# Scan core of a Mamba-2 layer: exponents four heads ahead, token tiles turned among the states

## The chip, the cores and the metric

The kernel runs on one core of one Trainium2 chip. The metric is the device time of one execution in microseconds (us), median of three runs; less is better. Engines are called PE (TensorE, matmuls and transposes), DVE (VectorE), ACT (ScalarE), POOL (GpSimd) and SP (SyncE, which here only issues DMAs). Each engine works through its own instructions in the order in which they are written; engines wait for one another by semaphores.

## What is computed

The program is a two-layer backbone over 256 latent tokens and 256 context tokens of width 1024 with SwiGLU feed-forward blocks around a mixer. The change lies in the mixer of the second layer alone, a bidirectional Mamba-2 scan:

```
x, B, C, dt = project(a)                 # 2048, 8*128, 8*128, 64 columns
a_cs        = cumsum(dt * A)             # per head and direction, 32 heads
cb          = C @ B^T                    # per group (8 groups of 4 heads), token x token
y_diag      = (cb * exp(segsum(a))) @ x  # inside the latent tokens
states      = B^T @ (x * decay_to_end)   # of the context tokens, carried over
y_off       = C @ states * exp(a_cs)
y           = y_diag + y_off + D * x     # then gated, normed, projected
```

## The kernel before

All arithmetic is fp32; large projections are split into a high and a low part. The program is written out engine by engine, and each engine's order is fixed by hand. The part around the change is called the core here, and has two parts.

**Ahead of the heads (L2157 to L2197 on PE).** `turn_x(x)` turns one tile of x (four 128x128 transposes) into a bank; tiles 0 to 7 are context, 8 to 15 latent tokens. `turn_b` does the same for B. DVE's `token_major(x)` (L1553) scales a turned tile twice, once for each direction, into `xtok`. `states(c4)` (L2152) makes the context states of two of the eight groups, and ACT copies them out to `ssb` (L978). Tiles 8 to 15 overwrite the place of tiles 0 to 7, so `token_major(8 + i)` waits for the states that read tile i. `b_dot_c(g)` (L2180, L2181) is B times C of a group; DVE masks two quarters of it (L1566, L1567). In the order before, all eight groups of states come first, then tiles 8 and 9 and B times C of group 0; tiles 10 to 15 are turned in the first three groups of heads, one for each pair.

**The heads (L2198 to L2226 on PE).** 32 heads in 8 groups of 4, two heads (a pair) at a time, 16 pairs. For a head h

- SP loads two rows of decays, each broadcast to 128 partitions (256 KB): `afb` (L591), from which the exponents are made, and `csx` (L582; by the buffer's name also `tt` or `pp`), which carries the states.
- DVE's `exponents(h)` makes two quarters `dm` from `afb` (L1577, L1578). It runs two heads ahead: `exponents(h + 2)` follows `products(h)`.
- ACT takes four exponentials into `ee` (L1006 to L1012).
- DVE's `products(h)` multiplies them with B times C (L1588, L1589) into `mm`, and then, once in a group, multiplies y of the group before with its gate (`gate_y`, L1600).
- POOL multiplies `csx` with C (L1741).
- PE adds for each pair D times x (L2206), the states (L2211) and the products (L2217 to L2223) in one bank; after the first pair of a group it makes B times C of the next group and sums squares of an earlier one (L2189).

Buffers: four `afb`, two `dm`, four `ee`, four `mm`, eight `csx`. SP's queue holds the two kinds of rows in turns: after `afb` of head h comes `csx` of head h + 3 (`CS_AHEAD = 3`). A `csx` row from head 8 on takes the buffer of head h - 8, and so waits until PE has done L2211 of that head's pair (`cs_used`, counted in pairs):

```
def decay_rows(h):
    if h >= 2 * HPG:
        sp.wait_ge(cs_used, h // 2 - HPG + 1)
    sp.dma_start(csx[cs_slot(h)]...)
```

An `afb` row from head 4 on waits for exponents and exponentials of head h - 4 (`d_done`, `e_done`).

Of the kernel before, what the change touches and what calls it, by code (L numbers as in the profile page):

```python
# [5 lines left out]
F32 = mybir.dt.float32  # L6
# [123 lines left out]
def build(nc, t, out, kscr, afscr, cscr):  # L130
# [39 lines left out]
    with ExitStack() as ctx:  # L170
# [17 lines left out]
        def sem(name):  # L188
            return ctx.enter_context(nc.semaphore(name))
# [63 lines left out]
        mm_ = [core(f"mm{i}", [3 * L]) for i in range(HPG)]  # L253
        afb = [core(f"afb{i}", [2, L]) for i in range(HPG)]
        dm = [core(f"dm{i}", [2 * P]) for i in range(2)]
        mask = core("mask", [3, P])
        btok = at("btok", [P, 2, D], F32, o_w)
        tt = [sb(f"tt{i}", [NT]) for i in range(4)]
# [134 lines left out]
        s_mask = sem("s_mask")  # L393
        afb_in = [sem(f"afb_in{i}") for i in range(HPG)]
        cb_mm = sem("cb_mm")
# [41 lines left out]
        def turned_x(x):  # L437
            return x % 4 if x < 8 else 0 if x == 8 else 7

# [11 lines left out]
        def _(sp):  # L451
# [135 lines left out]
            for h in range(HEADS):  # L587
                if h >= HPG:
                    sp.wait_ge(d_done, h - 3)
                    sp.wait_ge(e_done, h - 3)  # L590
                sp.dma_start(afb[h % HPG][:], afscr[0, h].partition_broadcast(P)).then_inc(afb_in[h % HPG], 16)  # L591
                if h + CS_AHEAD < HEADS:
                    decay_rows(h + CS_AHEAD)

            begin(MBOUT)
            for j in range(DT):
                sp.wait_ge(w_lo, MBOUT.w - 1 + j)
                if j == 1:
                    sp.wait_ge(cs_used, HEADS // 2 - 2)
                load(MBOUT.raw + j, mbo_v[:, :, j * P:j * P + P], 16, P)  # L600
# [15 lines left out]
        def _(act):  # L616
# [353 lines left out]
            for b in range(4):  # L970
                act.wait_ge(tb_mm, b + 1)
                if b == 0:
                    act.dma_start(mask[:].rearrange("p a n -> p (a n)"), t["c_mask"]).then_inc(s_mask, 16)
                act.activation(btok[:, b // 2, (b % 2) * 512:(b % 2) * 512 + 512], bank[6 + b % 2][:],
                               ACT.Copy).then_inc(tb_out, 1)
            for g in range(GROUPS):
                act.wait_ge(st_mm, g + 1)
                act.activation(ssb[:, :, g * 256:g * 256 + 256], bank[4 + g % 2][:].rearrange("p (a n) -> p a n", a=2),  # L978
                               ACT.Copy).then_inc(st_out, 1)
            act.wait_ge(af_st, 64)  # L980

# [13 lines left out]

            d_x(0)
            for h in range(HEADS):
                g, r = h // HPG, h % HPG
                d_ = dm[h % 2]
                if r == 1 and g + 1 < GROUPS:  # L1000
                    d_x(g + 1)
                act.wait_ge(afb_in[r], 16 * g + 16)
                if g:
                    act.wait_ge(m_done, h - 3)

                act.activation(ee[r][:, P:2 * P], afb[r][:, 0, P:L], ACT.Exp, bias=tk[:, 0, h:h + 1])  # L1006
                act.activation(ee[r][:, 2 * P:3 * P], afb[r][:, 1, 0:P], ACT.Exp, bias=tk[:, 1, HEADS + h:HEADS + h + 1])
                if g and r == 3:
                    square_y(g)
                act.wait_ge(d_done, h + 1)  # L1010
                act.activation(ee[r][:, 0:P], d_[:, 0:P], ACT.Exp, bias=tk[:, 0, HEADS + h:HEADS + h + 1])
                act.activation(ee[r][:, 3 * P:4 * P], d_[:, P:2 * P], ACT.Exp,  # L1012
                               bias=tk[:, 1, HEADS + h:HEADS + h + 1]).then_inc(e_done, 1)
            act.activation(rs[:, 24:25], eps[:], ACT.Sqrt)
            act.wait_ge(raw_in[MBOUT.raw % 2], 16 * (MBOUT.raw // 2 + 1))
# [27 lines left out]
        def _(dve):  # L1043
# [526 lines left out]
            def exponents(h):  # L1570

                g, r = h // HPG, h % HPG
                af, d_ = afb[r], dm[h % 2]
                dve.wait_ge(afb_in[r], 16 * g + 16)
                if h >= 2:
                    dve.wait_ge(e_done, h - 1)
                dve.scalar_tensor_tensor(d_[:, 0:P], af[:, 0, 0:P], tkd[:, 0, h:h + 1], af[:, 1, 0:P], ALU.add, ALU.min)  # L1577
                dve.scalar_tensor_tensor(d_[:, P:2 * P], af[:, 0, P:L], tkd[:, 1, h:h + 1], af[:, 1, P:L],  # L1578
                                         ALU.add, ALU.min).then_inc(d_done, 1)
# [26 lines left out]
            own.sync()  # L1606
            exponents(0)
            exponents(1)
            token_major(8)
            token_major(9)  # L1610
            b_dot_c(0)
            for h in range(HEADS):
                products(h)
                g, r = h // HPG, h % HPG
                if r % 2 and g < 3:
                    token_major(10 + 2 * g + r // 2)
                if r == 1 and g:
                    gate_y(g)
                if h + 2 < HEADS:
                    exponents(h + 2)  # L1620
                if r == 2 and g + 1 < GROUPS:
                    b_dot_c(g + 1)
# [40 lines left out]
        def _(pool):  # L1663
# [88 lines left out]
        def _(pe):  # L1752
# [377 lines left out]
            def turn_x(x):  # L2130

                seg, c4, T = 1 - x // 8, x % 8 // 2, x % 2
                if x >= 10:
                    pe.wait_ge(tr_out, x)
                elif x >= 4:
                    pe.wait_ge(tr_out, x - 3)
                elif T == 0:
                    pe.wait_ge(z_free, ZP.zf + 14 + x)
# [22 lines left out]
            pe.wait_ge(tb_out, 4)  # L2161
            for c4 in range(4):
                if 1 <= c4 < 3:
                    turn_x(2 * c4 + 2)
                    turn_x(2 * c4 + 3)
                states(c4)
            turn_x(8)
            turn_x(9)
            pe.wait_ge(st_out, GROUPS)
            pe.wait_ge(tk_out, 1)  # L2170

            def b_dot_c(g):

                if g:
                    pe.wait_ge(cb_out, g)
                whole = bank[1 + g % 2]
                for T in range(2):
# [182 lines left out]
```

## Time and profile before

| | us |
|---|---|
| median of 3 runs (lowest, highest) | 2005.96 (2005.37, 2007.53) |
| span of the profiled execution | 2002.1 |
| core ahead of the heads, in that span | 1644 to 1671.7 |
| the heads, in that span | 1671.7 to 1741 |

The profiled execution is told by its span, first instruction to last; the median of the runs is 3.9 us above it, which is what lies around the span and what runs differ by. Times of single instructions below are starts in us from the span's start. A matmul's duration is partly modelled and overlaps the next one's, so work on PE is measured from start to start. In an instruction row, xN is the count that was merged, and the bracket tells idle time of the engine ahead of it and what ended it.

### The profile page before, as it was taken

To read this page: it belongs to the slowest core of one execution; us is meant where nothing else is said; L and a number is where in the kernel's file an instruction comes from. 1 tells how busy PE (TensorE), PEld (TensorE's weight loads), DVE (VectorE), ACT (ScalarE), POOL (GpSimd) and SP (SyncE) were. 2 spreads that over 40 slices of the span, in tenths; PEclk is the share of its full clock that TensorE was granted. 3 is DMA by queue.
4 is the path that set the end of the run, shared out by engine and by line. 5 is a ranking of instruction groups with operands and counts; after the bars stand their busy time and mean duration, and the time that the engine had idled before them with its cause. 6 is when DMAs were issued, how large, how long until landed. Compare 5 with 4: busy or idle time off the path is not lost. (4 is left out here: it accounts for less than half of the span.)

```text
span 2002.1 us, 24595 instructions
## 1 busy us (share of the span) xinstructions
PE 1956.0 (98%) x9953; PEld 1631.5 (81%) x9953; DVE 1288.1 (64%) x1797; ACT 715.2 (36%) x1007; POOL 212.0 (11%) x151
## 2 busy tenths in 40 slices
PE   7999999999999999999999999999999998999998
PEld 4788888878888878888888888888888996688897
DVE  5755546678788576554767555466776578947654
ACT  4522222242311332223224222222434545735542
POOL 1000000100065200000110000001000003530001
PEclk9999999999999999999999999999999999999999
DMA  9544435543440254442655443355443445655554
GB/s 365 203 150 147 132 107 179 166 151 106 169 163 1 84 189 145 150 147 80 197 154 174 152 147 128 111 174 171 141 139 114 147 143 163 207 169 169 189 161 135
DMA packets 279302, 306.46 MB, mean 153 GB/s; under 512 B 9459, under 2 KB 249748, under 8 KB 277398
## 3 DMA queue, kind: packets, MB, share of 16 engines
q1 hardware_dynamic: 275398, 293.57, 46.0%
q10 hardware_dynamic: 3792, 11.33, 1.5%
q8 instruction: 78, 1.28, 0.3%
q14 instruction: 34, 0.28, 0.0%
HBM read 298.44 MB, written 6.43 MB: 152 GB/s over the span
## 5 line engine op out<-in xcount | busy, mean ns | idle before, releaser
L1756 PE MATMUL banks<-xhl,wh 128*128 128x512 f32 (+1 forms) x1756 | 664.9, 379 | 6.8 <-DVE xhl L1129 2.4
L1758 PE MATMUL banks<-xhl,wl 128*128 128x512 f32 (+1 forms) x1756 | 662.2, 377 | 0.0
L1757 PE MATMUL banks<-xhl,wh 128*128 128x512 f32 (+1 forms) x1756 | 662.1, 377 | 0.0
L1049 DVE TENSOR_TENSOR wl<-raw,wh 128x2048 fp32r<-128x2048 f32 (+2 forms) x193 | 398.7, 2066 | 236.8 <-ACT wh L622 231.5
L622 ACT ACTIVATE wh<-raw 128x2048 fp32r<-128x2048 f32 (+1 forms) x200 | 347.1, 1735 | 538.6 <-PE banks L1758 477.8
L1756 PEld LDWEIGHTS banks<-xhl,wh 128*128 128x128 f32 x1756 | 331.1, 189 | 75.7 <-DVE xhl L1129 5.7
L1758 PEld LDWEIGHTS banks<-xhl,wl 128*128 128x128 f32 x1756 | 331.0, 188 | 60.7
L1757 PEld LDWEIGHTS banks<-xhl,wh 128*128 128x128 f32 x1756 | 331.0, 189 | 59.2
L1756 PE MATMUL banks<-gh,wh 128*128 128x512 f32 (+1 forms) x704 | 255.4, 363 | 3.8 <-DVE wl L1049 3.8
L1757 PE MATMUL banks<-gl,wh 128*128 128x512 f32 (+1 forms) x704 | 255.2, 362 | 0.0
L1758 PE MATMUL banks<-gh,wl 128*128 128x512 f32 (+1 forms) x704 | 255.2, 362 | 0.0
L1194 DVE TENSOR_TENSOR pp<-tt,banks 128x512 f32<-128x512 f32 x66 | 42.4, 684 | 173.0 <-PE banks L1758 173.0
L1756 PEld LDWEIGHTS banks<-gh,wh 128*128 128x128 f32 x704 | 132.9, 189 | 24.9 <-issue 2.5
L1758 PEld LDWEIGHTS banks<-gh,wl 128*128 128x128 f32 x704 | 132.9, 189 | 20.7
L1757 PEld LDWEIGHTS banks<-gl,wh 128*128 128x128 f32 x704 | 132.9, 189 | 20.4
L1674 POOL MEMSET acc<- 128x512 f32 x6 | 3.2, 529 | 1150.7 <-DVE gl L1163 905.7
L1762 PE MATMUL banks<-xhl,wh 128*128 128x512 f32 x348 | 121.5, 396 | 0.8 <-DVE xhl L1129 0.8
L1680 POOL TENSOR_TENSOR acc<-acc,tt 128x512 f32<-128x512 f32 (+1 forms) x41 | 83.4, 2034 | 365.4 <-ACT tt L745 303.2
L695 ACT ACTIVATE tt<-banks 128x512 f32<-128x512 f32 x66 | 35.9, 596 | 239.3 <-PE banks L1758 239.2
L1763 PE MATMUL banks<-xhl,wl 128*128 128x256 f32 x348 | 96.5, 277 | 0.0
L1148 DVE SCALAR_TENSOR_TENSOR hT<-banks,mods,hT 128x256 f32<-128x256 f32 x64 | 28.7, 480 | 101.6 <-PE banks L1758 101.6
L1063 DVE SCALAR_TENSOR_TENSOR banks<-ada_rawo,cb 128x1024 f32<-128x1024 f32 x48 | 81.8, 1705 | 3.4 <-DMA ada_rawo<-in_ada_rest 3.4
(281 smaller groups left out, 2069.9 us busy)
## 6 DMA issues: line engine op xcount, KB each, us to landing
raw<-in_ffn_in SPq DMA_DIRECT2D x88, 1024.0 KB, 5.1
raw<-in_ffn_out SPq DMA_DIRECT2D x64, 704.0 KB, 4.6
ada_rawf<-in_ada_rest SPq DMA_DIRECT2D x60, 512.0 KB, 3.4
ada_rawo<-in_ada_rest SPq DMA_DIRECT2D x48, 512.0 KB, 3.3
raw<-in_mb_in_w SPq DMA_DIRECT2D x24, 1024.0 KB, 5.4
raw<-in_hy_in_w SPq DMA_DIRECT2D x12, 1024.0 KB, 5.2
afb<-decays SPq DMA_DIRECT2D x32, 256.0 KB, 3.8
raw<-in_mb_out_w SPq DMA_DIRECT2D x8, 1024.0 KB, 6.1
```

What stands on the lines that cost most here:

```text
L622: return act.activation(wh[n % 2][:, 0:cols], raw[r_slot][:, 0:cols], ACT.Copy).then_inc(w_hi, 1)
L695: act.activation(tt[u][:, 0:n], bank[u][:, 0:n], ACT.Silu).then_inc(gate_ready, 1)
L1049: dve.tensor_tensor(wl[n_slot][:, 0:cols], raw[r_slot][:, 0:cols], wh[n_slot][:, 0:cols].bitcast(F32), ALU.subtract).then_inc(w_lo, 1)
L1063: own(dve.scalar_tensor_tensor(banks[free][:].rearrange("p a n -> p (a n)"), pieces[i][:], half, cb0[:], ALU.mult, ALU.mult, accum_out=mod ...
L1148: ins = dve.scalar_tensor_tensor(x, bank[4 + um][:, w * L:w * L + L], mods[layer][:, i * 2 + (DT * k5 + um), w:w + 1], x, ALU.mult, ALU.add)
L1194: dve.tensor_tensor(pp[(pi.q + u) % 2][:, 0:n], tt[u][:, 0:n], acc[:, u * n:u * n + n] if n == L else bank[2 + u][:, 0:n], ALU.mult).then_ ...
L1680: pool.tensor_tensor(acc[:, 0:n], acc[:, 0:n], tt[um][:, 0:n], ALU.add).then_inc(acc_done, 1)
L1756: pe.matmul(dst, h, x_hi, start=start, stop=False)
L1757: pe.matmul(dst, h, x_lo, start=False, stop=False)
L1758: return pe.matmul(dst, l_, x_hi, start=False, stop=stop)
L1762: pe.matmul(b[:, 0:2 * L], wh[wslot][:, lo:lo + P], xhl[:, :, k, 0:L], start=k == 0, stop=False)
L1763: return pe.matmul(b[:, 0:L], wl[wslot][:, lo:lo + P], xh[:, k, 0:L], start=False, stop=k == DT - 1)
```

## The change

- `afb` gets eight buffers and `dm` four. `exponents(0)` to `exponents(3)` come ahead of the heads, and `exponents(h + 4)` follows `products(h)`. An `afb` row waits for head h - 8 instead of h - 4; the row of head 4 waits until tile 7 of x is turned, since its buffer lies where context x stood. `CS_AHEAD` and SP's order of rows stay.
- PE turns tiles 8 to 13 and makes B times C of group 0 among the states; only tiles 14 and 15 are left in group 0 of the heads. DVE scales them in the same order. Banks of the turned tiles and the waits for them change with it (`BANK_READ`).
- ACT takes the exponentials of head 0 and `d_x(0)` before the last two copies of states. POOL's `csx` product waits for the exponents of head h instead of h - 2, which is the same place in DVE's order.
- `btok` stands in a `raw` buffer, so the first load of the output projection waits for the last states.

```diff
         afb = [core(f"afb{i}", [2, L]) for i in range(HPG)]
+        afb += [at(f"afb{HPG + i}", [P, 2, L], F32, big + (24 + 2 * i) * KB) for i in range(HPG)]
         dm = [core(f"dm{i}", [2 * P]) for i in range(2)]
+        dm += [at(f"dm{2 + i}", [P, 2 * P], F32, big + (32 + i) * KB) for i in range(2)]
...
-        btok = at("btok", [P, 2, D], F32, o_w)
+        btok = at("btok", [P, 2, D], F32, o_raw + MBOUT.raw % 2 * 8 * KB)
...
         def turned_x(x):
-            return x % 4 if x < 8 else 0 if x == 8 else 7
+            return x % 4 if x < 8 else (0, 7, 2, 7, 0, 2, 7, 7)[x - 8]
+
+        BANK_READ = {8: 5, 10: 7, 11: 10, 12: 9, 13: 11, 14: 12, 15: 15}
...
             for h in range(HEADS):
-                if h >= HPG:
-                    sp.wait_ge(d_done, h - 3)
-                    sp.wait_ge(e_done, h - 3)
-                sp.dma_start(afb[h % HPG][:], afscr[0, h].partition_broadcast(P)).then_inc(afb_in[h % HPG], 16)
+                if h == HPG:
+                    sp.wait_ge(tr_mm, 8)
+                if h >= 2 * HPG:
+                    sp.wait_ge(d_done, h - 7)
+                    sp.wait_ge(e_done, h - 7)
+                sp.dma_start(afb[h % (2 * HPG)][:], afscr[0, h].partition_broadcast(P)).then_inc(afb_in[h % (2 * HPG)], 16)
                 if h + CS_AHEAD < HEADS:
                     decay_rows(h + CS_AHEAD)
...
+                if j == 0:
+                    sp.wait_ge(st_mm, GROUPS)
...
+            exponentials(0)
+            state_out(GROUPS - 2)
+            d_x(0)
+            state_out(GROUPS - 1)
+            for h in range(1, HEADS):
+                exponentials(h)
...
             def exponents(h):
-                dve.wait_ge(afb_in[r], 16 * g + 16)
-                if h >= 2:
-                    dve.wait_ge(e_done, h - 1)
+                dve.wait_ge(afb_in[h % (2 * HPG)], 16 * (h // (2 * HPG)) + 16)
+                if h >= HPG:
+                    dve.wait_ge(e_done, h - 3)
...
-            exponents(0)
-            exponents(1)
+            for h in range(HPG):
+                exponents(h)
             token_major(8)
             token_major(9)
+            token_major(10)
+            token_major(11)
             b_dot_c(0)
+            token_major(12)
+            token_major(13)
             for h in range(HEADS):
                 products(h)
                 g, r = h // HPG, h % HPG
-                if r % 2 and g < 3:
-                    token_major(10 + 2 * g + r // 2)
+                if r % 2 and g == 0:
+                    token_major(14 + r // 2)
                 if r == 1 and g:
                     gate_y(g)
-                if h + 2 < HEADS:
-                    exponents(h + 2)
+                if h + HPG < HEADS:
+                    exponents(h + HPG)
...
-                    pool.wait_ge(d_done, h - 1)
+                    pool.wait_ge(d_done, h + 1)
...
-            for c4 in range(4):
-                if 1 <= c4 < 3:
-                    turn_x(2 * c4 + 2)
-                    turn_x(2 * c4 + 3)
-                states(c4)
-            turn_x(8)
-            turn_x(9)
-            pe.wait_ge(st_out, GROUPS)
-            pe.wait_ge(tk_out, 1)
+            states(0)
+            turn_x(4)
+            turn_x(5)
+            states(1)
+            for x in range(6, 10):
+                turn_x(x)
+            states(2)
+            turn_x(10)
+            turn_x(11)
...
             b_dot_c(0)
+            states(3)
+            turn_x(12)
+            turn_x(13)
+            pe.wait_ge(st_out, GROUPS)
+            pe.wait_ge(tk_out, 1)
...
-                    if g < 3:
-                        turn_x(10 + 2 * g + p)
+                    if g == 0:
+                        turn_x(14 + p)
```

What the change makes of the order on two engines follows. First SP's queue from the row of head 3 on, before (L591 is `afb`, L582 the other kind; the names number the buffers):

```order
L591 DMA afb3_108<-decays 128x512
L582 DMA pp0_119<-decays 128x512
L591 DMA afb0_105<-decays 128x512 [waits e_done,d_done]
L582 DMA pp1_120<-decays 128x512
L591 DMA afb1_106<-decays 128x512 [waits e_done,d_done]
L582 DMA csx0_121<-decays 128x512 [waits cs_used]
L591 DMA afb2_107<-decays 128x512 [waits e_done,d_done]
L582 DMA csx1_122<-decays 128x512 [waits cs_used]
L591 DMA afb3_108<-decays 128x512 [waits e_done,d_done]
```

and the same stretch after (L597 is `afb`, L586 the other kind):

```order
L597 DMA afb3_108<-decays 128x512
L586 DMA pp0_125<-decays 128x512
L597 DMA afb4_109<-decays 128x512 [waits tr_mm]
L586 DMA pp1_126<-decays 128x512
L597 DMA afb5_110<-decays 128x512
L586 DMA csx0_127<-decays 128x512 [waits cs_used]
L597 DMA afb6_111<-decays 128x512
L586 DMA csx1_128<-decays 128x512 [waits cs_used]
L597 DMA afb7_112<-decays 128x512
```

The rows of heads 4 to 7 lose their waits for earlier heads; the place of every row, and the wait for `cs_used` ahead of head 6, stay.

DVE at heads 3 to 5, before (L1588 and L1589 are the products, L1577 and L1578 the exponents, L1553 a tile of x):

```order
L1588 TENSOR_TENSOR mm3_104<-ee3_100,banks0 128x512 [waits e_done,cb_out]
L1589 TENSOR_TENSOR mm3_104<-ee3_100,banks1 128x256
L1553 TENSOR_TENSOR xtok_53<-banks3,tk_155 128x512 [waits tr_mm,st_mm]
L1553 TENSOR_TENSOR xtok_53<-banks3,tk_155 128x512
L1577 SCALAR_TENSOR_TENSOR dm1_110<-afb1_106,tkd_156 128x128 [waits e_done,afb_in1]
L1578 SCALAR_TENSOR_TENSOR dm1_110<-afb1_106,tkd_156 128x128
L1588 TENSOR_TENSOR mm0_101<-ee0_97,banks1 128x512 [waits head_mm,e_done,cb_out]
L1589 TENSOR_TENSOR mm0_101<-ee0_97,banks1 128x256
L1577 SCALAR_TENSOR_TENSOR dm0_109<-afb2_107,tkd_156 128x128 [waits e_done,afb_in2]
L1578 SCALAR_TENSOR_TENSOR dm0_109<-afb2_107,tkd_156 128x128
L1588 TENSOR_TENSOR mm1_102<-ee1_98,banks1 128x512 [waits head_mm,e_done,cb_out]
```

and after (L1606 and L1607, L1595 and L1596, L1572):

```order
L1606 TENSOR_TENSOR mm3_104<-ee3_100,banks0 128x512 [waits e_done,cb_out]
L1607 TENSOR_TENSOR mm3_104<-ee3_100,banks1 128x256
L1572 TENSOR_TENSOR xtok_53<-banks3,tk_161 128x512 [waits tr_mm,st_mm]
L1572 TENSOR_TENSOR xtok_53<-banks3,tk_161 128x512
L1595 SCALAR_TENSOR_TENSOR dm3_116<-afb7_112,tkd_162 128x128 [waits e_done,afb_in7]
L1596 SCALAR_TENSOR_TENSOR dm3_116<-afb7_112,tkd_162 128x128
L1606 TENSOR_TENSOR mm0_101<-ee0_97,banks1 128x512 [waits head_mm,e_done,cb_out]
L1607 TENSOR_TENSOR mm0_101<-ee0_97,banks1 128x256
L1595 SCALAR_TENSOR_TENSOR dm0_113<-afb0_105,tkd_162 128x128 [waits e_done,afb_in0]
L1596 SCALAR_TENSOR_TENSOR dm0_113<-afb0_105,tkd_162 128x128
L1606 TENSOR_TENSOR mm1_102<-ee1_98,banks1 128x512 [waits head_mm,e_done,cb_out]
```

Between the products of heads 4 and 5 now stand the exponents of head 8, which read the row in `afb0`; before it was those of head 6.

## Rows read from the trace of the kernel before

**Rows 1.** The page's section 1, busy time of each engine
```profile
PE 1956.0 (98%) x9953; PEld 1631.5 (81%) x9953; DVE 1288.1 (64%) x1797; ACT 715.2 (36%) x1007; POOL 212.0 (11%) x151
```

**Rows 2.** Busy time by stage, over the heads; columns in the first line
```profile
core 0: us, PE busy (x) PEld busy (x) DVE busy (x) ACT busy (x) POOL busy (x), PEclk, DMA share, GB/s
...
1667.00:1740.00 73.00, 65.53 (x544) 42.87 (x544) 68.01 (x161) 53.73 (x153) 35.76 (x28) 0.98 0.70 220
```

**Rows 3.** Timeline of PE, heads: start, us, engine, line, op
```profile
1682.68 0.65 PE L2217 MATMUL banks<-mm,xtok 128*64 128x256 f32 x4 [1.06 <-DVE mm L1589]
...
1703.18 0.65 PE L2217 MATMUL banks<-mm,xtok 128*64 128x256 f32 x4 [1.37 <-DVE mm L1589]
...
1718.85 0.65 PE L2217 MATMUL banks<-mm,xtok 128*64 128x256 f32 x4
...
1723.63 0.60 PE L2217 MATMUL banks<-mm,xtok 128*64 128x256 f32 x4
...
1725.03 0.70 PE L2206 MATMUL banks<-xb,small 128*128 128x256 f32 x2
1725.66 1.08 PE L2211 MATMUL banks<-csx,ssb 128*64 128x256 f32 x8
1726.67 0.65 PE L2217 MATMUL banks<-mm,xtok 128*64 128x256 f32 x4
...
1728.12 0.49 PE L2180 MATMUL banks<-csb,xb 128*128 128x128 f32 x2
...
1729.93 0.68 PE L2206 MATMUL banks<-xb,small 128*128 128x256 f32 x2
```

**Rows 4.** Timeline of DVE: exponents 25, products 24, exponents 26, exponents 28
```profile
1723.26 0.34 DVE L1577 SCALAR_TENSOR_TENSOR dm<-afb,tkd 128x128 f32<-128x128 f32 x1
...
1723.78 0.68 DVE L1588 TENSOR_TENSOR mm<-ee,banks 128x512 f32<-128x512 f32 x1
...
1724.71 0.72 DVE L1577 SCALAR_TENSOR_TENSOR dm<-afb,tkd 128x128 f32<-128x128 f32 x1
...
1728.59 0.72 DVE L1577 SCALAR_TENSOR_TENSOR dm<-afb,tkd 128x128 f32<-128x128 f32 x1
```

**Rows 5.** Timeline of SP: the decays of head 30, then afb of head 28
```profile
1723.84 0.32 SPq L582 DMA_DIRECT2D pp<-decays  x1
1724.26 0.42 SPq L591 DMA_DIRECT2D afb<-decays  x1
```

**Rows 6.** Waits of SP's queue, 1640 to 1742: total, times, longest
```profile
SPq L582 <- PE banks L2211: 16.5, 10, 2.9
```

**Rows 7.** Transfers into afb, from issue to landing
```profile
DMA to landing us min/median/max: 3.1/3.8/7.1
```

**Rows 8.** Timeline of PE, ahead of the heads and at the first pair
```profile
1656.99 7.07 PE L2152 MATMUL banks<-xtok,btok 128*128 128x256 f32 x32
1663.90 1.04 PE L2140 MATMUL banks<-small,xb 128*128 128x128 f32 x8
1664.77 0.47 PE L2180 MATMUL banks<-csb,xb 128*128 128x128 f32 x2
...
1665.74 0.60 PE L2206 MATMUL banks<-xb,small 128*128 128x256 f32 x2
...
1671.67 1.12 PE L2217 MATMUL banks<-mm,xtok 128*64 128x256 f32 x4 [2.77 <-DVE mm L1589]
...
1674.43 0.80 PE L2180 MATMUL banks<-csb,xb 128*128 128x128 f32 x2
```

**Rows 9.** Timeline of DVE, ahead of the heads
```profile
1659.15 0.34 DVE L1577 SCALAR_TENSOR_TENSOR dm<-afb,tkd 128x128 f32<-128x128 f32 x1
...
1664.61 2.48 DVE L1553 TENSOR_TENSOR xtok<-banks,tk 128x512 f32<-128x512 f32 x4 [4.32 <-PE banks L2140]
1667.01 0.43 DVE L1566 TENSOR_TENSOR banks<-banks,mask 128x256 f32<-128x256 f32 x1
```

**Rows 10.** Busy time by stage, columns as in rows 2
```profile
1672.00:1673.00 1.00, 1.00 (x8) 0.65 (x6) 1.00 (x4) 0.25 (x1) 0.00 (x0) 0.50 0.76 203
```

More of the change, by code:

```diff
@@ L393, in build @@
         s_mask = sem("s_mask")
-        afb_in = [sem(f"afb_in{i}") for i in range(HPG)]
+        afb_in = [sem(f"afb_in{i}") for i in range(2 * HPG)]
         cb_mm = sem("cb_mm")
@@ L972, in _ @@
                 if b == 0:
+                    act.wait_ge(w_lo, ZP.w + 7)
                     act.dma_start(mask[:].rearrange("p a n -> p (a n)"), t["c_mask"]).then_inc(s_mask, 16)
@@ L975, in _, with state_out @@
                                ACT.Copy).then_inc(tb_out, 1)
-            for g in range(GROUPS):
+            def state_out(g):
                 act.wait_ge(st_mm, g + 1)
@@ L979, in _ @@
                                ACT.Copy).then_inc(st_out, 1)
+            for g in range(GROUPS - 2):
+                state_out(g)
             act.wait_ge(af_st, 64)
@@ L994, in d_x, with exponentials @@
                     act.activation(xb[:, 0, m, :], xb[:, 0, m, :], ACT.Copy, scale=dcol[:, m:m + 1]).then_inc(dx_done, 1)
-            d_x(0)
-            for h in range(HEADS):
+            def exponentials(h):
                 g, r = h // HPG, h % HPG
-                d_ = dm[h % 2]
+                d_, af = dm[h % HPG], afb[h % (2 * HPG)]
                 if r == 1 and g + 1 < GROUPS:
                     d_x(g + 1)
-                act.wait_ge(afb_in[r], 16 * g + 16)
+                act.wait_ge(afb_in[h % (2 * HPG)], 16 * (h // (2 * HPG)) + 16)
                 if g:
                     act.wait_ge(m_done, h - 3)
-                act.activation(ee[r][:, P:2 * P], afb[r][:, 0, P:L], ACT.Exp, bias=tk[:, 0, h:h + 1])
-                act.activation(ee[r][:, 2 * P:3 * P], afb[r][:, 1, 0:P], ACT.Exp, bias=tk[:, 1, HEADS + h:HEADS + h + 1])
+                act.activation(ee[r][:, P:2 * P], af[:, 0, P:L], ACT.Exp, bias=tk[:, 0, h:h + 1])
+                act.activation(ee[r][:, 2 * P:3 * P], af[:, 1, 0:P], ACT.Exp, bias=tk[:, 1, HEADS + h:HEADS + h + 1])
                 if g and r == 3:
@@ L1570, in exponents @@
             def exponents(h):
-                g, r = h // HPG, h % HPG
-                af, d_ = afb[r], dm[h % 2]
-                dve.wait_ge(afb_in[r], 16 * g + 16)
-                if h >= 2:
-                    dve.wait_ge(e_done, h - 1)
+                af, d_ = afb[h % (2 * HPG)], dm[h % HPG]
+                dve.wait_ge(afb_in[h % (2 * HPG)], 16 * (h // (2 * HPG)) + 16)
+                if h >= HPG:
+                    dve.wait_ge(e_done, h - 3)
                 dve.scalar_tensor_tensor(d_[:, 0:P], af[:, 0, 0:P], tkd[:, 0, h:h + 1], af[:, 1, 0:P], ALU.add, ALU.min)
@@ L2132, in turn_x @@
                 seg, c4, T = 1 - x // 8, x % 8 // 2, x % 2
-                if x >= 10:
-                    pe.wait_ge(tr_out, x)
-                elif x >= 4:
+                if x in BANK_READ:
+                    pe.wait_ge(tr_out, BANK_READ[x])
+                elif 4 <= x < 8:
                     pe.wait_ge(tr_out, x - 3)
-                elif T == 0:
+                elif x < 4 and T == 0:
                     pe.wait_ge(z_free, ZP.zf + 14 + x)
@@ L2175, in b_dot_c @@
                     pe.wait_ge(cb_out, g)
+                if g == 1:
+                    pe.wait_ge(tr_out, 14)
                 whole = bank[1 + g % 2]
```

## The prediction

> **What bounds the kernel now.** I read the page from its first section down. PE is busy 98% of the span [rows 1], so the program as a whole is bound by its matmuls, and almost no saving on another engine can show outside the few stretches in which PE waits. The core is one. Over the heads the stage table has PE at 65.5 and DVE at 68.0 of 73.0 us, ACT at 53.7, POOL at 35.8 [rows 2]: two engines nearly full, so neither the mean nor the busiest engine says what bounds it. The timelines do. From pair 10 to pair 12, one group of heads, PE takes 1726.67 - 1718.85 = 7.82 us with no idle bracket in its rows [rows 3]. In the early groups it takes longer: pair 2 to pair 6 are (1703.18 - 1682.68) / 2 = 10.25 us a group, and there PE waits for DVE's products, as the brackets of 1.06 and 1.37 us tell [rows 3]. What DVE has more in the first three groups is two tiles of x a group. One pair of tiles costs DVE 1667.01 - 1664.61 = 2.40 us, 1.20 each [rows 9]. So the early groups are bound by DVE, the late ones by DVE and PE alike, and 2.40 of the 10.25 us is what the change takes aim at.
>
> Behind both stands a third party, SP's queue. It spent 16.5 us, in 10 waits, on PE's state matmuls L2211 [rows 6], since the `csx` rows wait for them, and every `afb` row waits its turn behind a `csx` row. Today that costs nothing, and how narrowly is seen at head 28: the state matmuls of pair 11 end when its products start, at 1723.63 [rows 3]; SP issues the decays of head 30 at 1723.84 and `afb` of head 28 at 1724.26 [rows 5]; a median landing of 3.8 us later [rows 7] is 1728.06; DVE reads it at 1728.59 [rows 4]. 0.5 us is to spare.
>
> **The change part by part.** I write T(k) for the start of pair k's products on PE.
>
> *Ahead of the heads.* DVE makes four heads' exponents in place of two before tile 8: it starts them at 1659.15 [rows 9], one head is 1723.78 - 1723.26 = 0.52 us [rows 4], so it is free at 1661.2 in place of 1660.2, and tile 9 is scaled at 1663.6. PE needs that for tile 11 (its bank), then makes B times C of group 0 (1665.74 - 1664.77 = 0.97), two groups of states (a quarter of 1663.90 - 1656.99 each, 1.73, so 3.46) and turns tile 12 (an eighth matmul row of 0.87 for two, 0.44) [rows 8]: 1663.6 + 0.44 + 0.97 + 3.46 + 0.44 = 1668.9. DVE then scales tiles 12 and 13 (2.40), and makes products 0, exponents 4, products 1. Products are 1724.71 - 1723.78 = 0.93 [rows 4], so T(0) = 1668.9 + 2.40 + 0.93 + 0.52 + 0.93 = 1673.7, against 1671.67 [rows 8]: **+2.0 us**. ACT's reordered work (head 0's exponentials before the last copies) lies under the states, and costs nothing unless the copies delay PE; a copy is short against the 1.73 us of a state group.
>
> *Group 0 of the heads.* Before, T(0) to T(2) is 1682.68 - 1671.67 = 11.0 us [rows 3, 8]. After, DVE has four heads of 0.93 + 0.52, two tiles of 1.20, two masks (an estimate of 0.66, from 0.43 for one [rows 9] less what overlaps), and about 0.38 twice, where L1577 takes 0.72 and not 0.34 [rows 4]: 5.8 + 2.4 + 0.66 + 0.76 = 9.6 us, and behind it a first wait for `afb` of head 8 of up to 1 us, by the same sum as below. **-0.5 us**, between -1.4 and +2.
>
> *Groups 1 to 7, the term that decides.* Two tiles a group less in groups 1 and 2 would save 2.4 us each. But moving exponents two heads up in DVE's order, without moving the `afb` rows up in SP's, moves the reader before the transfer. Exponents 28 should now follow products 24, at 1724.71 [rows 4], while the row lands at 1728.1. Behind it in DVE's queue stand products 25, and PE's pair 12 waits for those. The loop that closes is: state matmuls of pair k end; +0.21 and +0.42 until SP has issued `csx` and started `afb` of head 2k + 6 [rows 3, 5]; +3.8 to landing [rows 7]; +0.52 exponents, +0.93 products of head 2k + 3 [rows 4]; so T(k + 1) comes 5.9 us after. Then PE's products of a pair, 1728.12 - 1726.67 = 1.45, B times C and sum of squares, 1729.93 - 1728.12 = 1.81, and D times x and states of pair k + 2, 1726.67 - 1725.03 = 1.64 [rows 3], and the next loop begins. Together **10.8 us a group**, against 7.82. (This holds for odd k, whose T(k + 1) opens a group; for even k PE has reached its states early enough, while it waited, that nothing is added.)
>
> In groups 1 and 2, before 10.25 each, the saved tiles and the new wait cancel: 10.8 each, less 0.8 of the 1.81 once, because only from group 2 on squares are summed: **+0.3 us** for both. From T(6) to T(12), three groups, it is 3 x (10.8 - 7.82) = **+8.9 us**. I temper it to +8, because a stretched loop has fewer transfers in flight and the landing then tends to its minimum, 3.1 us [rows 7]: the bounds are 10.1 us a group, +6.8, and 10.8, +8.9. After T(12) exponents are done but for heads 30 and 31, and nothing is added or saved.
>
> The Trainium skill, in "DMA: Bandwidth & Descriptors" (Anatomy of one DMA), has a fixed cost of about 2.0 us and then bytes by 436 GB/s, an estimate of 2.6 us for 256 KB; by that the loop were 9.6 us and this term +5.3. The landing that the profile has, 3.8 with a minimum of 3.1, decides.
>
> *TensorE's clock.* Ahead of T(0) PE is idle for 2.77 us [rows 8], and right after the granted clock is 0.50, the 1.2 GHz level [rows 10]: pair 0's products take 1674.43 - 1671.67 = 2.76 in place of 1.45. After, every group holds 10.8 - 7.8 = 3 us of idle in one piece, ahead of its first pair. One such fall costs 1.3 us in the products and some 0.4 in what follows; between none and one in each of six groups, 0 to +9; I take two: **+3 us**. The Trainium skill describes this in "TensorE: Matmul & The Clock Gate" (HAM oscillation): a loop whose matmuls are short beside the transfer wait finds the clock low in every round. By that it would be six falls, a rival below.
>
> *The rest.* The first load of the output projection, at 1729 before, can only come earlier; its reader comes after the heads. POOL's product stays at the same place of DVE's order. `btok` in another buffer and the banks cost nothing. All that follows the heads moves with them.
>
> **The sum**: 2.0 - 0.5 + 0.3 + 8 + 3 = +12.8 us on the span of 2002.1, so 2014.9, and with the 3.86 us by which the median of the runs lies above the span, 2018.8.
>
> **Rivals.**
> 1. *Faster: the tiles' time shows and the rows are in time.* The place is groups 1 and 2, 2 x 2.4 = 4.8 us less, group 0 -1.4, ahead of the heads +2.0: -4.2, 2001.8. For it: PE did wait there for DVE. It decides if the new wait costs less than 4.2 / 3 = 1.4 us in each of the last three groups, which needs landings within about 2.2 us of issue, or `afb` issued 1.6 us sooner. Against: the minimum of 32 is 3.1. Chance 0.06.
> 2. *No change.* The two cancel, with a gain of some 4 us given back: 2006. It needs the in-between of the above. 0.05.
> 3. *The clock falls in every group*: 2.0 - 0.5 + 0.3 + 8 + 9 = +18.8, 2024.8. For it: idle pieces of 3 us, where 2.77 sufficed once. Against: with 1.06 and 1.37 us nothing fell, and part of a fall hides in the wait that follows. 0.24.
> 4. *The clock never falls, and landings are short*: 2.0 - 1.0 - 0.5 + 6.8 = +7.3, 2013.3. 0.20.
> 5. *The change doesn't do what it says*: eight `afb` buffers don't bring rows earlier, because `cs_used` gates the queue. That is part of my forecast.
>
> **How the numbers follow.** Forecast 2018.8 with 0.45; rivals 3 and 4 with 0.24 and 0.20; 0.11 for the first two. The range goes from 2011, a little under rival 4, to 2026, a little over rival 3. About 4 us, 0.2%, is what a measurement of this kernel can tell from no change. Slower by more than that 0.89, same 0.05, faster 0.06.
>
> **What would show it.** Right: DVE idle ahead of L1595 until a DMA into `afb` lands, 2 to 4 us once a group from group 2 on; PE idle ahead of L2246 by some 3 us at the first pair of a group; T(6) to T(12) some 32 us in place of 23.5; T(0) near 1673.7; SP's waits for L2240 far over 16.5 us. Wrong: no DVE wait for a DMA, or a group of heads at 7.8 us. Were T(0) to T(6) shorter by 4 us and the rest unchanged, rival 1 holds.

## The result, and the profile after

| | before | changed |
|---|---|---|
| median on one chip, 6 runs each (lowest, highest), us | 2005.66 (2003.67, 2007.53) | 2019.48 (2014.87, 2026.96) |
| ratio, with its 95% interval | | 1.0075 (1.0058 to 1.0092) |
| span of the profiled execution (its run) | 2002.1 | 2015.6 (2017.41) |

The change makes the kernel slower, by 13.8 us (0.69%) between the medians and by 0.75% by the ratio. The forecast was 2018.8 in 2011 to 2026. All ratios are of fast runs alone: one slow execution of the kernel before, 3281.98 us at a granted clock of 0.56, taken beside experiments 1 to 4, is not in them.

Line numbers have moved. On PE the products are L2246 (L2217 before), the states L2240 (L2211), D times x L2235 (L2206), turned x L2162 (L2140), sum of squares L2213 (L2189). On DVE exponents are L1595 (L1577), products L1606 and L1607 (L1588, L1589), scaled tiles L1572 (L1553). On SP `afb` is L597 (L591), `csx` L586 (L582).

The page's section 1 of the changed kernel, against [rows 1]:

```profile
PE 1961.2 (97%) x9953; PEld 1637.0 (81%) x9953; DVE 1285.8 (64%) x1797; ACT 713.7 (35%) x1007; POOL 212.1 (11%) x151
```

Counts are the same. Of the 13.5 us by which the span grew, PE was busy for 5.2 (1961.2 for 1956.0), with the same matmuls, and idle for 8.3 (a matmul's duration is partly modelled). So what was added is waiting, and matmuls that took longer. Busy time by stage of the changed kernel, over the stretch of [rows 2]:

```profile
core 0: us, PE busy (x) PEld busy (x) DVE busy (x) ACT busy (x) POOL busy (x), PEclk, DMA share, GB/s
...
1667.00:1740.00 73.00, 56.63 (x420) 36.45 (x418) 51.08 (x126) 40.73 (x127) 30.62 (x24) 0.91 0.52 172
```

PE did 544 matmuls in these 73 us before and now 420, DVE 68.0 us of work and now 51.1. No engine is near full. Even the DMA engines move less, 172 GB/s in place of 220, so neither bandwidth nor an engine's own work took the time. PE's timeline, the first product row of pairs 0, 2, 6, 8, 9, 10, 11, 12 and 15, against [rows 3, 8]:

```profile
1672.81 0.65 PE L2246 MATMUL banks<-mm,xtok 128*64 128x256 f32 x4 [2.47 <-DVE mm L1607]
...
1684.52 0.65 PE L2246 MATMUL banks<-mm,xtok 128*64 128x256 f32 x4 [2.36 <-DVE mm L1607]
...
1705.75 0.65 PE L2246 MATMUL banks<-mm,xtok 128*64 128x256 f32 x4 [3.19 <-DVE mm L1607]
...
1716.34 0.65 PE L2246 MATMUL banks<-mm,xtok 128*64 128x256 f32 x4 [2.70 <-DVE mm L1607]
...
1721.14 0.65 PE L2246 MATMUL banks<-mm,xtok 128*64 128x256 f32 x4
...
1726.94 0.65 PE L2246 MATMUL banks<-mm,xtok 128*64 128x256 f32 x4 [2.63 <-DVE mm L1607]
...
1735.03 1.07 PE L2246 MATMUL banks<-mm,xtok 128*64 128x256 f32 x4
...
1741.04 0.65 PE L2246 MATMUL banks<-mm,xtok 128*64 128x256 f32 x4 [1.36 <-DVE mm L1607]
...
1752.82 0.60 PE L2246 MATMUL banks<-mm,xtok 128*64 128x256 f32 x4
```

Pair 10 to pair 12 took 7.82 us before with no bracket. Now pair 6 to 8 takes 1716.34 - 1705.75 = 10.59, pair 8 to 10 10.60, pair 10 to 12 14.10, and each opens with idle time that DVE's products end. Why DVE is late is seen in its own timeline, and beside it in SP's and PE's, around pair 8.

DVE:

```profile
1711.28 0.41 DVE L1607 TENSOR_TENSOR mm<-ee,banks 128x256 f32<-128x256 f32 x1
1714.75 0.35 DVE L1595 SCALAR_TENSOR_TENSOR dm<-afb,tkd 128x128 f32<-128x128 f32 x1 [3.06 <-DMA afb<-decays]
...
1715.28 0.68 DVE L1606 TENSOR_TENSOR mm<-ee,banks 128x512 f32<-128x512 f32 x1
```

SP:

```profile
1710.74 0.32 SPq L586 DMA_DIRECT2D pp<-decays  x1
1711.16 0.38 SPq L597 DMA_DIRECT2D afb<-decays  x1
```

PE:

```profile
1709.62 1.08 PE L2240 MATMUL banks<-pp,ssb 128*64 128x256 f32 x8
1710.53 0.60 PE L2246 MATMUL banks<-mm,xtok 128*64 128x256 f32 x4
```

Pair 7's states end when its products start, at 1710.53; 0.21 later SP issues the `csx` row that waited for them, 0.42 later `afb` of head 20. DVE stands from 1711.7 on in exponents 20, with products 17 behind them, until the row lands 3.6 us after its issue. PE's pair 8 starts 1.59 after that. T(8) - T(7) (T(k) is the start of pair k's products) is 5.81 us for the 5.9 forecast, and T(9) - T(8) is 4.80 for 1.45 + 1.81 + 1.64 = 4.90. The loop is the forecast's, term by term. Waits over the heads of the changed kernel (total, times, longest), DVE's and PE's:

```profile
DVE dm L1595 <- DMA afb<-decays: 19.2, 10, 5.5
PE banks L2246 <- DVE mm L1607: 17.4, 9, 3.2
```

and SP's, against [rows 6]:

```profile
SPq L586 <- PE banks L2240: 57.5, 12, 12.8
```

All three changed as foretold; SP waited 16.5 us for the states before. But SP's wait is a weak sign: it is also 39.5 and 38.0 us in experiments 1 and 7 below, in which nothing is lost. With eight `afb` buffers SP hardly waits for the exponentials any more (38.8 us before), and spends the time on the states. Of the three, DVE's wait for `afb` and PE's wait for DVE tell late rows from early ones.

What remains is the third group, 14.10 us. PE at pair 11, and the granted clock of that stretch:

```profile
1732.14 1.20 PE L2235 MATMUL banks<-xb,small 128*128 128x256 f32 x2
1733.27 1.98 PE L2240 MATMUL banks<-pp,ssb 128*64 128x256 f32 x8
```

```profile
1728.00:1738.00 10.00, 10.00 (x49) 6.75 (x45) 4.98 (x13) 5.62 (x19) 3.82 (x3) 0.50 0.28 90
```

The granted clock is 0.50, the lower level, 1.2 GHz; ahead of pair 10 PE had been idle for 2.63 us. The states take 1.98 in place of 1.08. Pair 10 to 11 takes 8.09 us where pair 8 to 9 took 4.80: 3.3 us, once. SP stands behind those states too, so `afb` of head 28 goes out at 1735.71 and DVE's wait is the longest of all:

```profile
1735.71 0.38 SPq L597 DMA_DIRECT2D afb<-decays  x1
```

```profile
1739.44 0.35 DVE L1595 SCALAR_TENSOR_TENSOR dm<-afb,tkd 128x128 f32<-128x128 f32 x1 [5.49 <-DMA afb<-decays]
```

### The profile page after: what moved, and what is told of

Read it like the earlier page. It is cut to its first block, busy times and chain, and to the rows that moved or that the text cites. A ratio compares the mean times of both kernels' runs of the same rounds, so it can differ in the third digit from the quotient of the medians.

```text
span 2015.6 us, 24591 instructions
## 1 busy us (share of the span) xinstructions
PE 1961.2 (97%) x9953; PEld 1637.0 (81%) x9953; DVE 1285.8 (64%) x1797; ACT 713.7 (35%) x1007; POOL 212.1 (11%) x151
## 4 chain that ended last, share of the span: by engine, by line
PE 60%; DVE 3%; DMA 2%; ACT 1%; issue 1%; POOL 0%; SPq 0%; DVEq 0%; ACTq 0%
PE banks L1778 17%; PE banks L1779 17%; PE banks L1780 17%; PE banks L1784 4%; PE banks L1785 2%; DMA afb<-decays 1%; DMA raw<-in_ffn_out 1%; DVE wl L1068 1%; ACT wh L630 1%; PE banks L2174 1%; PE banks L2240 0%; DVE xhl L1148 0%; PE banks L1823 0%; DMA raw<-in_mb_out_w 0%; PE banks L2246 0%
## 5 line engine op out<-in xcount | busy, mean ns | idle before, releaser
L1780 PEld LDWEIGHTS banks<-gh,wl 128*128 128x128 f32 x704 | 132.9, 189 | 20.7
```

Source lines behind the costliest of these rows:

```text
L1780: return pe.matmul(dst, l_, x_hi, start=False, stop=stop)
```

## The experiments

The theory: the reader of a row (exponents, on DVE) was moved two heads up and the row that it reads was not, because its place in SP's queue is set by `CS_AHEAD` and not by the number of buffers. The rivals: the tiles among the states cost the time, or the eight buffers and waits as such, or the low clock does. Each ratio is taken against the kernel before on the same chip. The stages of all profiled executions stand in one table, in us; each row is one execution. The first stage counts from SP's first `csx` issue, 1644.17 before and 1642.72 after, since the core starts at other times of the span. The distance is worked out from the code: `CS_AHEAD` - 1 plus the number of heads by which exponents run ahead. The larger it is, the later a row is issued as seen from its reader.

| kernel | distance | to T(0) | T(0) to T(2) | to T(6) | to T(12) | to T(15) |
|---|---|---|---|---|---|---|
| before | 2 + 2 | 27.5 | 11.0 | 20.5 | 23.5 | 11.7 |
| changed | 2 + 4 | 30.1 | 11.7 | 21.2 | 35.3 | 11.8 |
| e1_rows_early | 0 + 4 | 30.1 | 10.9 | 15.7 | 23.9 | 11.6 |
| e2_tiles_only | 2 + 2 | 29.0 | 9.6 | 15.7 | 23.8 | 11.7 |
| e3_exps_only | 2 + 4 | 27.5 | 11.1 | 20.7 | 35.8 | 13.2 |
| e4_before_rows_late | 4 + 2 | 27.5 | 12.0 | 23.7 | 38.1 | 13.2 |
| e5_kept_busy | 2 + 4 | 30.1 | 11.0 | 20.9 | 33.7 | 14.5 |
| e6_early_late_exps | 0 + 4 | 29.0 | 10.9 | 15.7 | 23.9 | 11.9 |
| e7_tiles_rows_early | 0 + 2 | 29.0 | 9.6 | 15.7 | 23.5 | 11.7 |
| e8_kept_busy_1_to_6 | 2 + 4 | 30.1 | 12.4 | 21.0 | 33.6 | 11.6 |
| e9_rows_one_early | 1 + 4 | 31.8 | 9.6 | 16.0 | 26.0 | 11.9 |

**1. The rows moved up too.** The changed kernel, with

```diff
-        CS_AHEAD = 3
+        CS_AHEAD = 1
```

> The changed kernel with CS_AHEAD = 1 in place of 3 and nothing else: SP issues each afb row two places earlier, ahead of the csx rows that wait for PE. Theory (an afb row lands too late because it stands behind a csx row): DVE's waits for afb, 19.2 us in all after the change, fall under 2 us, the last three groups from T(6) to T(12) take 23.5 us again in place of 35.3, and the time is 2003 us (2001 to 2005), 16 us under the changed kernel and 2 to 3 under the one before. Rival (the loss comes from the order on DVE and PE itself, or from the exponents' place, and the rows are only seen last): the time stays above 2014. Rival (csx rows, now issued later, become the new late ones): DVE's waits vanish, PE's L2240 waits for POOL take their place, and the time is between 2008 and 2016.

2000.14 us (12 runs, 1996.10 to 2002.95), ratio 0.9981 (0.9972 to 0.9990): the whole loss is gone with one constant, and a little of a gain stands. PE's timeline of this kernel, pairs 6 and 12:

```profile
1700.92 0.65 PE L2246 MATMUL banks<-mm,xtok 128*64 128x256 f32 x4
...
1724.84 0.65 PE L2246 MATMUL banks<-mm,xtok 128*64 128x256 f32 x4
```

and its waits of DVE for `afb`, 1.5 us where the changed kernel has 19.2:

```profile
DVE dm L1595 <- DMA afb<-decays: 1.5, 4, 0.6
```

Place and cause are as expected. The time is 0.9 us under the range of 2001 to 2005, on a chip on which the kernel before is 2.0 us faster as well (2003.66 for 2005.66). Tiles, buffers and exponents are still as in the changed kernel, and so don't cause the loss among the heads.

**2. The tiles alone.** The changed kernel with exponents two ahead, as before; POOL's `csx` product keeps its place in DVE's order by waiting two heads less.

```diff
-            for h in range(HPG):
+            for h in range(2):
                 exponents(h)
...
-                if h + HPG < HEADS:
-                    exponents(h + HPG)
+                if h + 2 < HEADS:
+                    exponents(h + 2)
...
-                    pool.wait_ge(d_done, h + 1)
+                    pool.wait_ge(d_done, h - 1)
```

> The changed kernel with exponents two heads ahead again, SP's queue as it is: only the tiles of x and B times C among the states are left of the change. Theory: exponents are read 2 heads later, when their row has landed; groups 1 and 2 save two tiles of 1.20 us each, ahead of the heads it costs about 1.5 us, so 2002 us (2000 to 2004), 3 to 4 us under before. Rival (moving the tiles is what costs, since PE and DVE wait for each other ahead of the heads): 2008 or more.

1998.06 us (8 runs, 1994.50 to 2000.45), ratio 0.9970 (0.9959 to 0.9980). Pairs 2 and 6 on PE:

```profile
1681.46 0.65 PE L2246 MATMUL banks<-mm,xtok 128*64 128x256 f32 x4 [1.32 <-DVE mm L1607]
...
1697.13 0.65 PE L2246 MATMUL banks<-mm,xtok 128*64 128x256 f32 x4
```

15.67 us in place of 20.50: 4.8 us less, just the four tiles at 1.20 of the forecast's first rival. Group 0 gives 1.4 more and the core ahead of the heads takes 1.5. The ratio is a gain of 0.30%, some 6 us, more than the 3 to 4 expected. This half of the change is good, and the other half buried it.

**3. The exponents alone.** The kernel before with eight `afb`, four `dm` and exponents four ahead; tiles as before.

```diff
+        afb += [at(f"afb{HPG + i}", [P, 2, L], F32, big + (24 + 2 * i) * KB) for i in range(HPG)]
         dm = [core(f"dm{i}", [2 * P]) for i in range(2)]
+        dm += [at(f"dm{2 + i}", [P, 2 * P], F32, big + (32 + i) * KB) for i in range(2)]
...
-                if h >= HPG:
-                    sp.wait_ge(d_done, h - 3)
-                    sp.wait_ge(e_done, h - 3)
...
+                if h == HPG:
+                    sp.wait_ge(tr_mm, 8)
+                if h >= 2 * HPG:
+                    sp.wait_ge(d_done, h - 7)
+                    sp.wait_ge(e_done, h - 7)
...
-            exponents(0)
-            exponents(1)
+            for h in range(HPG):
+                exponents(h)
...
-                if h + 2 < HEADS:
-                    exponents(h + 2)
+                if h + HPG < HEADS:
+                    exponents(h + HPG)
```

> The kernel before with eight afb and four dm buffers and the exponents four heads ahead, tiles of x where they were. Theory: the same late rows, but groups 1 and 2 still have their tiles, during which rows land; the time is 2017 us (2011 to 2022), 10.6 us or more a group from T(6) to T(12). Rival (tiles): within 2 us of before, 2006.

2017.43 us (6 runs, 2011.02 to 2020.74), ratio 1.0064 (1.0046 to 1.0082): the loss by itself, as expected. DVE's wait is there with its tiles in the old place:

```profile
DVE dm L1581 <- DMA afb<-decays: 14.2, 8, 6.3
```

Pair 2 to 6 takes 20.7 us, hardly more than before (20.5): there the tiles fill DVE's time while the rows land, and its waits for `afb` are 0.15 and 0.50 us. The loss shows only from pair 6 on.

**4. The loss without the change.** The kernel before, exponents two ahead, with

```diff
-        CS_AHEAD = 3
+        CS_AHEAD = 5
```

> The kernel before with CS_AHEAD = 5: nothing moves on PE, DVE, ACT or POOL, only each afb row stands two places later in SP's queue. Theory: that alone makes the same wait, since it sets the same distance between a row and its reader: DVE waits for afb, a group of heads takes 10.6 us, the time is 2017 us (2011 to 2022). Rival (the place in the queue is not what decides, the buffers and orders of the change do): unchanged, 2006.

2022.48 us (5 runs, 2020.33 to 2026.23), ratio 1.0101 (1.0088 to 1.0115). Here no buffer, tile or reader is moved, only the row. Its waits for `afb`:

```profile
ACT ee L1006 <- DMA afb<-decays: 22.6, 10, 4.5
DVE dm L1577 <- DMA afb<-decays: 17.5, 8, 4.3
```

So it is the distance in the table that counts, whichever side is moved. At 2 and 4 pair 6 to 12 takes 23.5 to 23.9 us, at 6 it takes 33.6 to 38.1. The size was missed: 2017 in 2011 to 2022 was expected, with 10.6 us a group, and the three groups took 12.0, 12.9 and 13.1. PE's idle pieces ahead of pairs 8, 10 and 12 are 4.08, 3.58 and 3.63 us, longer than in the changed kernel, and after two of them the granted clock is 0.50 (1719 to 1721, 1732 to 1734). How much each of the two adds was not tried.

**5. PE kept busy while it waits.** The changed kernel, with six matmuls into a bank that nobody reads at that time, ahead of the wait that opens groups 1 to 7 (their result is not used). It asks what the low clock is worth.

```diff
+                    if g and p == 0:
+                        pe.wait_ge(tr_out, 16)
+                        for c in range(6):
+                            pe.matmul(bank[7][:, 0:L], ident, xb[:, 0, 2 * g, :], start=True, stop=True)
                     pe.wait_ge(m_done, g * HPG + 2 * p + 2)
```

> The changed kernel with six matmuls of 128x256, into a bank that nobody reads, ahead of PE's wait for the products of the first pair of groups 1 to 7: some 2.6 us of work in the idle piece of 2.4 to 3.2 us. The late afb rows stay. Theory (the rest of the loss over the late rows is TensorE's clock): no stretch at a granted clock of 0.50 between T(1) and T(12), T(6) to T(12) is 31.8 us (3 x 10.6) in place of 35.3, the time 2015 us (2013 to 2017), and runs lie closer together than the 12 us of the changed kernel. Rival (the stretch of 14.1 us is a late transfer of its own and not the clock): 35 us stay, and the spread too. The added matmuls may themselves cost up to 1 us where a piece is shorter than they are.

2018.67 us (5 runs, 2015.36 to 2021.01), ratio 1.0086 (1.0072 to 1.0100). The number expected, 2015 in 2013 to 2017, was missed. The granted clock did stay at 1.00, 2.4 GHz, over the heads:

```profile
1673.00:1750.00 77.00, 74.49 (x558) 51.64 (x556) 54.81 (x136) 43.58 (x128) 34.50 (x27) 1.00 0.59 188
```

but group 7 waited for nothing there, so its matmuls cost their full 2.7 us (14.5 in place of 11.8), and pair 6 to 8 took 1715.58 - 1703.46 = 12.1 us:

```profile
1703.46 0.65 PE L2250 MATMUL banks<-mm,xtok 128*64 128x256 f32 x4
...
1715.58 0.65 PE L2250 MATMUL banks<-mm,xtok 128*64 128x256 f32 x4 [1.43 <-DVE mm L1607]
```

since one `afb` row, issued at 1708.87, was only read at 1713.98, 5.1 us later, in place of 3.6.

**6. Rows early, and two of the first exponents late.** Experiment 1 with exponents 2 and 3 between B times C of group 0 and tile 12, where DVE stands idle for 2.54 us ahead of tile 12 in the changed kernel.

```diff
-            for h in range(HPG):
+            for h in range(2):
                 exponents(h)
...
             b_dot_c(0)
+            exponents(2)
+            exponents(3)
             token_major(12)
```

> The changed kernel with CS_AHEAD = 1, and with the exponents of heads 2 and 3 after tile 11 and the masks in place of ahead of tile 8: exponents still four heads ahead among the heads. Theory (four heads' exponents ahead of tile 8 hold up PE's tile 11 and with it T(0), 1.0 us of the 2.6 that the change lost there): T(0) comes 29.0 us after SP's first row in place of 30.1, and the time is 1999 us, 1 to 2 under the same kernel without that move. Rival: nothing moves, since the end is set by PE's sequence.

1997.45 us (11 runs, 1995.96 to 2002.43), ratio 0.9976 (0.9967 to 0.9985). T(0) comes 29.0 us after SP's first issue and not 30.1, as expected: two heads of exponents, 1.1 us, were on the path ahead of the heads. The 1 to 2 us expected against experiment 1 don't show in the time: the two ratios, 0.9981 and 0.9976, have intervals that overlap.

**7. The tiles, with rows early.** Experiment 2 with `CS_AHEAD = 1`.

> The kernel with only the tiles among the states (exponents two heads ahead), and CS_AHEAD = 1. Theory: with exponents two heads ahead the rows were in time but for 2.0 us of DVE's waits, so at most 0 to 1 us is gained: 1998 us (1996 to 2000). Rival (exponents four heads ahead gain something of their own once rows are in time): this kernel is slower than the one with exponents four heads ahead and rows early.

1997.61 us (10 runs, 1996.70 to 1999.66), ratio 0.9979 (0.9969 to 0.9988), in the range expected. DVE's list of waits has no wait for `afb` any more, where experiment 2 still has 0.6 us on DVE and 1.4 on ACT, and pair 6 to 12 is 23.5, as before. The time is not better for it: with a distance of 4 the rows are near enough in time, and more lead buys nothing that can be measured. Nor do exponents four ahead gain anything of their own, as 6 and 7 side by side tell.

**8. Kept busy in groups 1 to 6.** Experiment 5 without its group 7, against its kernel:

```diff
-                    if g and p == 0:
+                    if 0 < g < 7 and p == 0:
```

> The kernel kept busy ahead of the first pair of a group, but not in group 7, where the six matmuls cost 2.8 us because nothing is waited for there. Theory (low clock is a part of the loss, besides the late rows): T(12) to T(15) is 11.7 us again in place of 14.5, no stretch at 0.50 from T(1) to T(12), the median 2016 us (2013 to 2018), 2 to 4 under the changed kernel, and the runs within 7 us. Rival (low clock costs nothing, since the wait for the row hides it): the median is that of the changed kernel, 2019 to 2020.

2015.95 us (5 runs, 2012.07 to 2018.63), ratio 1.0068 (1.0055 to 1.0081). Group 7 is back at 11.6 (pair 12 to 15), as expected, and the clock is full:

```profile
1680.00:1754.00 74.00, 71.62 (x548) 49.32 (x546) 52.15 (x129) 41.02 (x120) 31.96 (x25) 1.00 0.60 193
```

PE's timeline, pairs 6, 8, 10 and 12, gives 12.17, 10.61 and 10.79 us a group:

```profile
1708.38 0.65 PE L2250 MATMUL banks<-mm,xtok 128*64 128x256 f32 x4
...
1720.55 0.65 PE L2250 MATMUL banks<-mm,xtok 128*64 128x256 f32 x4 [1.49 <-DVE mm L1607]
...
1731.16 0.65 PE L2250 MATMUL banks<-mm,xtok 128*64 128x256 f32 x4
...
1741.95 0.65 PE L2250 MATMUL banks<-mm,xtok 128*64 128x256 f32 x4
```

The loop stays with the clock full, so the low clock is not the cause of it. The ratio is not told apart from the changed kernel's 1.0075, whose interval overlaps, so the rival expectation, that the low clock costs nothing in the median, is not ruled out; this chip's before, 2001.54, is 4.1 us under the other's, and the time alone, which lies where the theory put it, would have flattered the kernel. The profile has 33.6 against 35.3 for pair 6 to 12: 1.7 us less, the fall of 3.3 gone and a late row of 1.5 in its place. That row shows in both kernels with the added matmuls and not in the changed one; whether they cause it was not tried.

**9. Rows one place early.** The changed kernel with `CS_AHEAD = 2`.

> The changed kernel with CS_AHEAD = 2: each afb row one place earlier in SP's queue. Since cs_used counts pairs of heads, the row of an even head then waits for one pair less, as with CS_AHEAD = 1, and the row of an odd head as before. Theory (the row of the even head, which closes the loop over the first pair of a group, is the late one): nearly the whole loss goes, 2000 us (1998 to 2004). Rival (every place in the queue counts alike): half of it stays, 2008 to 2013.

2001.73 us (12 runs, 1999.27 to 2006.71), ratio 1.0002 (0.9994 to 1.0011), in the range expected. One place is worth nearly all, and not half. DVE's waits for `afb` fall to a fifth:

```profile
DVE dm L1595 <- DMA afb<-decays: 3.8, 6, 1.2
```

In the changed kernel the row that DVE waits for once a group is that of an even head, which stands behind a fresh `cs_used`; a place up, it stands behind a `csx` row that waits for one pair less. At 26.0 us for pair 6 to 12 it is still 2 us over a distance of 4: at distance 5 the late rows begin to show, in this one kernel. So the distance does not count place by place; which row stands behind a fresh wait counts too. (Its T(0) is 1.7 us later than in the changed kernel, and T(0) to T(2) 2.1 shorter: the clock was low ahead of T(0) this time, and not at it.)

```profile
1664.00:1667.00 3.00, 3.00 (x9) 2.37 (x8) 1.34 (x4) 0.00 (x0) 0.00 (x0) 0.50 0.00 0
```

## Why the prediction was right, and where it was off

- **The median, 2018.8 for 2019.48, and the sign**: right. The span was to be 2014.9 and is 2015.6. The stages, less the 1.45 us by which this core starts earlier, add up: 2.6 + 0.7 + 0.7 + 11.8 + 0.1 - 0.9 (all that follows T(15)) - 1.45 = 13.5. That the number came so near is luck in two places. The stages up to T(15) add up to +15.9 where I had +12.8, and 0.9 + 1.45 us that no term of mine names took most of that back. And of the 3.86 us put on top of the span only 1.8 lies between a run and its own span (2017.41 and 2015.6); if that holds before too, the profiled execution there was 2 us faster than its median, and the changed kernel's happened to be so as well, by 2.1 us (2017.41 for 2019.48).
- **Groups 3 to 5, the term that decides**: right in cause and size. 10.8 us a group from rows of before; 10.59 and 10.60 where the clock held, 10.61 and 10.79 in experiment 8. At 10.6, three groups are 31.8, +8.3 over 23.5, for +8 taken; the other 3.5 of the 11.8 us lie in the stretch of low clock, below. The row of the loop took 3.6 and 3.7 us (1711.16 to 1714.75, 1735.71 to 1739.44) for 3.8. The shorter landing by which +8.9 was tempered to +8 shows in these rows but not over all: the median of the 32 rose to 4.3, and in experiments 1 and 7, where hardly a row is waited for, it is 5.0 and 4.9:

```profile
DMA to landing us min/median/max: 3.2/4.3/6.5
```

So that fewer transfers in flight land sooner, as I had it, is not shown. The Trainium skill's fixed part and bandwidth, "DMA: Bandwidth & Descriptors" (Anatomy of one DMA), gave 2.6; but that fit is stated for DMAs that GpSimd issues, and these rows are issued by SP, so it was the wrong line to take. No landing of any run here was under 3.1.
- **The clock, +3**: right in sum, by another split, and so by luck. Two falls of some 1.7 each had been taken; in this one execution it was a single stretch of 10.2 us (1728.0 to 1738.2) and cost 3.3. What rivals 3 and 4 hung on was the idle piece ahead of a group: after 2.63 us the clock fell, after 3.19 and 2.70 it didn't. So neither "in every group" nor "never" held. The six falls that I drew from the Trainium skill, "TensorE: Matmul & The Clock Gate" (HAM oscillation), don't follow from it: it tells of loops whose matmuls are shorter than the wait, and here a group has 7.8 us of matmuls beside some 3 us of idle. What the clock is worth in the median stays open: experiment 8 finds no difference.
- **Ahead of the heads, +2.0**: +2.6. The DVE part was right: exponents begin 15.0 us after SP's first issue in both kernels, and take 2.1 (1657.71 to 1659.81), as priced. What failed is the chain through PE, tile 9 to tile 12: start to start it came out 0.4 us longer. DVE starts on tile 12 at 1667.89, 0.7 after PE began to turn it (1667.18), and I had priced the turn (0.44) and no step from PE to DVE behind it.
- **Group 0, -0.5**: +0.7, inside its bounds of -1.4 to +2. DVE's work, 9.6 us, was priced right: that is what the stage takes in experiments 2, 7 and 9, in which the clock is full there and DVE waits for nothing. The changed kernel has one wait for `afb` in it, 1.01 us, as I had put it (the second, 0.59, ends after T(2)). What I had at nothing is the low clock after T(0), 0.57 from 1673 to 1677, though the rows of before show it: DVE waits 0.76 and 0.42 us for PE's B times C and turned tile. 9.6 + 1.0 + 1.2 = 11.8 for the 11.7 measured. Experiments 1 and 6 have a low clock there and no wait for `afb`, and take 10.9.
- **Groups 1 and 2, +0.3**: +0.7. That saved tiles and new wait cancel there was right, and experiments 1 and 2 show it: without the wait the stage is 15.7, with the wait and no tiles 21.2, with tiles and no wait (before) 20.5.
- **Rival 1** priced the tiles at -4.8 in groups 1 and 2 and -1.4 in group 0, and asked for `afb` 1.6 us sooner. Experiments 1, 2, 6 and 7 are that case: all of them are a little faster than before.
- **Rival 5**, that the buffers don't bring the row that decides any earlier, is shown by its issue: `afb` of head 20 leaves 0.63 us after T(7) in both kernels, at 1708.59 after 1707.96 before, at 1711.16 after 1710.53 now. With eight buffers and `CS_AHEAD = 3` the loss is there (3), and with the same eight and 1 it is not (1).

Four versions beat both kernels: tiles among the states with exponents two ahead (0.9970), the same with rows early (0.9979), exponents four ahead with rows early (0.9981), and that with two exponents late (0.9976), 0.2 to 0.3% under their own before. Their intervals overlap; the first is the simplest.

## What to carry to other kernels

A deeper buffer brings a transfer earlier only if the buffer was what held it; in an in-order queue look at which issue stands ahead of it, and what that one waits for. Count the lead as one distance, from the transfer's place in its queue to the reader's place in its own, and move both ends together. A change that gives with one part and takes with another is worth splitting: here 0.3% of gain (0.9970, experiment 2) was hidden under a loss. And the parts need not add up: alone the exponents cost 0.64% (experiment 3), on top of the tiles 1.05% (1.0075 / 0.9970). In groups 1 and 2 the exponents add 0.2 us where the tiles still stand (20.7 for 20.5) and 5.5 where they don't (21.2 for 15.7).

## What was not expected of the hardware

The granted clock can differ between executions that are alike. The changed kernel and experiments 5 and 8 are the same program up to group 1, and in each PE is idle for the same 2.47 us ahead of T(0); behind it the clock was low, full and low. Experiments 1, 2, 6, 7 and 9 have the same idle piece: low in 1 and 6, full in 2, 7 and 9. It is worth 1.3 us: with no wait for `afb`, T(0) to T(2) takes 9.6 us at the full clock and 10.9 after the low one. So stages of single profiles can differ by that much with nothing in the code to account for it.

The same row, issued behind the same waits, took 3.6 us in one kernel and 5.1 in another. What sets that, and the granted clock's choice between idle pieces of 2.5 and 3.2 us, these runs don't tell.

Nor do they tell whether a late row makes the kernel uneven. The changed kernel's 6 runs spread over 12.1 us (2014.87 to 2026.96) and the 6 of experiment 3 over 9.7. But the 5 of experiment 4, with the largest loss, spread over 5.9, and the kernel before itself over 3.9 in 6 runs and over 6.0 in each of the sets of 17 to 20 on the other chips.
